# A two-layer decoder trunk on one core: the order of work at the hand-overs between weight strips, and one value strip by the plain product

## The reference, cut to what matters

```python
mem_n = rmsnorm(mem, mem_norm)               # 256 memory tokens
for layer in range(2):
    h = rmsnorm(x, g[0])
    # layer 0: proj = h @ w_in -> q, k, v, u; stick-breaking attention on q, k, v (4 heads x 256),
    #          pooling mixer on u; both concatenated @ w_out
    # layer 1: proj = h @ w_in -> q, k, v, r, a; g = log_sigmoid(a @ gate_w + gate_b) / 16,
    #          gated linear attention in chunks of 64; its norm, times silu(r), @ w_out
    x = x + rmsnorm(mix, g[1])
    x = x + rmsnorm(cross_attention(rmsnorm(x, g[2]), mem_n, ...), g[3])    # 4 heads x 512
    x = x + rmsnorm((silu(h @ w_gate) * (h @ w_up)) @ w_down, g[5])         # h = rmsnorm(x, g[4])
```

## Time and profile before

| | before |
|---|---|
| median of three runs | 3054.8 us |
| the profiled execution, its own time | 3051.12 us |
| its span, first to last instruction | 3049.4 us |
| mean granted TensorE clock, as a share of 2.4 GHz | 0.978 |
| PE busy | 2901.0 us, 95% of the span |
| DVE busy | 2092.8 us, 69% |
| ACT busy | 1541.1 us, 51% |
| POOL busy | 99.6 us, 3% |
| HBM traffic | 191 GB/s over the span |

### The profile page before, as it was taken

How to read it: one execution, slowest core, us unless ns; L and a number is a source line. 1 busy time by engine, 2 the same in 40 slices (tenths; PEclk the granted TensorE clock), 3 DMA queues, 4 the chain that set the end, 5 groups by cost and what they waited for, 6 DMA issues and landing times. The chain is left out here.

```text
span 3049.4 us, 31694 instructions
## 1 busy us (share of the span) xinstructions
PE 2901.0 (95%) x13070; PEld 2398.4 (79%) x13070; DVE 2092.8 (69%) x1376; ACT 1541.1 (51%) x1361; POOL 99.6 (3%) x112
## 2 busy tenths in 40 slices
PE   6999999998899999999998969998999999999998
PEld 5888787787787888887887858777777888887887
DVE  6888776547447888885445858646645988886544
ACT  4666555445335566664444545444434655665443
POOL 0000000001001000000002000001001000000000
PEclk9999999999999999999999969999999999999999
DMA  7665744654454566556554424754535455665552
GB/s 262 221 255 183 279 155 149 235 172 140 184 166 168 205 221 221 192 183 260 193 193 155 166 82 156 262 207 150 195 138 193 178 184 205 221 221 203 211 193 97
DMA packets 237984, 583.44 MB, mean 191 GB/s; under 512 B 8720, under 2 KB 8736, under 8 KB 222096
## 3 DMA queue, kind: packets, MB, share of 16 engines
q1 hardware_dynamic: 232608, 530.61, 49.0%
q0 software_dynamic: 4064, 38.21, 3.2%
q10 hardware_dynamic: 1168, 12.59, 1.0%
HBM read 564.60 MB, written 16.78 MB: 191 GB/s over the span
## 5 line engine op out<-in xcount | busy, mean ns | idle before, releaser
L999 DVE TENSOR_TENSOR w_lo<-wide,w_hi 128x2048 fp32r<-128x2048 f32 x552 | 1255.9, 2289 | 529.7 <-ACT w_hi L542 527.9
L542 ACT ACTIVATE w_hi<-wide 128x2048 fp32r<-128x2048 f32 x552 | 1053.2, 1914 | 559.8 <-PE ps L1547 456.4
L1547 PE MATMUL ps<-w_hi,act_hi 128*128 128x512 f32 x3312 | 1215.4, 393 | 39.0 <-DVE act_lo L1141 22.5
L1547 PE MATMUL ps<-w_lo,act_hi 128*128 128x512 f32 x3312 | 1209.2, 391 | 0.0
L1547 PE MATMUL ps<-w_hi,act_lo 128*128 128x512 f32 x3312 | 1208.7, 391 | 0.0
L1547 PEld LDWEIGHTS ps<-w_hi,act_hi 128*128 128x128 f32 x3312 | 626.3, 189 | 175.5 <-issue 27.8
L1547 PEld LDWEIGHTS ps<-w_hi,act_lo 128*128 128x128 f32 x3312 | 625.4, 189 | 131.4
L1547 PEld LDWEIGHTS ps<-w_lo,act_hi 128*128 128x128 f32 x3312 | 626.3, 189 | 129.1 <-issue 0.2
L1003 DVE TENSOR_TENSOR wide<-wide,wide 128x2048 f32<-128x2048 f32 x108 | 247.2, 2289 | 5.5 <-DVE w_sum L1003 0.5
L1547 PE MATMUL ps<-w_hi,s_hi_x 128*128 128x512 f32 x544 | 217.5, 400 | 23.8 <-ACT ps L592 18.3
L1547 PE MATMUL ps<-w_hi,s_lo_x 128*128 128x512 f32 x544 | 214.4, 394 | 0.0
(11 more groups left out here) (211 smaller groups left out, 1424.6 us busy)
## 6 DMA issues: line engine op xcount, KB each, us to landing
wide<-in_ffn_w_gate SPq DMA_DIRECT2D x88, 1024.0 KB, 7.5
wide<-in_ffn_w_up SPq DMA_DIRECT2D x88, 1024.0 KB, 7.2
wide<-in_ffn_w_down SPq DMA_DIRECT2D x88, 1024.0 KB, 4.8
wide<-in_odd_w_in SPq DMA_DIRECT2D x48, 1024.0 KB, 5.2
wide<-in_xattn_wk SPq DMA_DIRECT2D x32, 1024.0 KB, 8.0
wide<-in_xattn_wv SPq DMA_DIRECT2D x32, 1024.0 KB, 7.0
wide<-in_even_w_in SPq DMA_DIRECT2D x32, 1024.0 KB, 7.1
wide<-in_xattn_wq SPq DMA_DIRECT2D x32, 1024.0 KB, 5.1
```

Source lines behind the costliest of these rows:

```text
L542: nc.scalar.activation(w_hi[:, c % W_SLOTS, :], src, ACT.Copy).then_inc(hi_done, 2)
L999: nc.vector.tensor_tensor(w_lo[:, c % W_SLOTS, :], src, w_hi[:, c % W_SLOTS, :].bitcast(F32), ALU.subtract).then_inc(lo_done, 2)
L1547: return nc.tensor.matmul(dst, lhs, rhs, start=start, stop=stop, skip_group_check=loose)
```

## The change

It does six things:

- The turn of the scale vectors becomes the first work of PE, and its copy the first of DVE.
- In the five stages that go through `transposed`, ACT takes both token halves of a plain strip (`take_both`). In all seven stages the token additions move behind the low part of chunk 7, and `token_hi` and `token_lo` behind chunk 0 of the next strip.
- The scores of the first mixer move inside `sb_vu`'s first strip, behind its chunk c+3. ACT's copies of them come ahead of c+9, Abs to Ln behind c+10, and DVE's join behind chunk 0 of the next strip. The last turn of `sb_qk` moves behind that strip's chunk c.
- `gla_v`'s first strip becomes plain. `state_gates` comes behind chunk 0 of the second strip and `chunk_forms` behind its chunk 3.
- The last `take_t` of `xq` moves ahead of chunk 3 of the next strip (`closes`).
- `band` less one moves ahead of c+7 of `sb_vu`'s first strip on DVE.

```diff
@@ the plan
+    stage("vec", rounds=1)
     stage("mem_norm", rounds=2)
...
-    stage("vec", rounds=1)
...
-            stage("gla_v", (True, True))
+            stage("gla_v", (False, True))
@@ ACT
+            def take_both(st, q, reuse=()):
+                def run():
+                    for m in range(MT):
+                        if m == 0:
+                            act.wait_ge(m0_done, st.a + q + 1)
...
+                        else:
+                            act.wait_ge(w_used, st.c + 4 * q + 4 + W_SLOTS)
+                        nc.scalar.activation(nat[:, q, m, :], ps[:, 2 * q + m, :], ACT.Copy)\
+                            .then_inc(bank_free[2 * q + m], 1)
+                return run
...
-                        rest8(st, before_5, take_m0(st, 0, nat[:, 0, 0, :], reuse=reuse(0)))
-                        if i == 0 and name in SUM_STAGES:
-                            token_hi(name)
-                        lead(nx, take_t(0), take_m0(st, 1, nat[:, 1, 0, :], reuse=reuse(1)))
+                        rest8(st, before_5, take_both(st, 0, reuse(0)))
+                        lead(nx, lambda: (token_hi(name), take_t(0)()), take_both(st, 1, reuse(1)))
...
-                             take_t(0))
+                             (lambda: (take_t(0)(), take_t(1)())) if closes and i == 1 else take_t(0))
...
+                    natural(vu_strips[0], vu, 0, vu_strips[1], take_k, before_9=scores, at_end=soft_plus)
...
-                    natural(v_strips[0], gv, 0, v_strips[1], exp_state)
+                    natural(v_strips[0], gv, 0, v_strips[1], before_1=exp_state)
...
-                token_hi(f"gu{l}")
-                lead(gu[1])
+                lead(gu[1], lambda: token_hi(f"gu{l}"))
@@ DVE
-                            rest8(st, before_5, lambda: (token_adds(name, token_free(name)), own()))
-                            token_lo(name)
...
-                        lead(nx, take_t(0), take_m1(st, 1, nat[:, 1, 1, :], reuse(1)))
+                        rest8(st, before_5)
+                        token_adds(name, token_free(name))
+                        lead(nx, lambda: (token_lo(name), take_t(0)()))
...
+                if st.g is None:
+                    rest8(st, before_5, take_m1(st, 0, dst[:, 1, col:col + NB]))
+                    lead(nxt, before_1, take_m1(st, 1, dst[:, 1, right]))
+                    at_end()
+                    return
...
             first = strip_of("mk0")
+            dve.wait_ge(work_full[4], plan["vec"]["rf"] + 1)
+            nc.vector.tensor_copy(vec[:], ps[:, 4, 0:16]).then_inc(vec_done, 1)
...
-                    transposed("sb_qk", qk, vu_strips[0])()
-                    dve.wait_ge(l_done, 1)
...
+                    take_k = transposed("sb_qk", qk, vu_strips[0])
...
+                    natural(vu_strips[0], vu, 0, vu_strips[1], take_k, band_less_one, soft_plus)
...
-                    natural(v_strips[0], gv, 0, v_strips[1], state_gates, chunk_forms)
+                    natural(v_strips[0], gv, 0, v_strips[1], before_1=state_gates, at_end=chunk_forms)
...
-                rest8(gu[0], before_7=lambda: token_adds(f"gu{l}", token_free(f"gu{l}")))
-                token_lo(f"gu{l}")
-                lead(gu[1], before_3=times_up)
+                rest8(gu[0])
+                token_adds(f"gu{l}", token_free(f"gu{l}"))
+                lead(gu[1], lambda: token_lo(f"gu{l}"), times_up)
@@ PE
             pe.wait_ge(consts_done, 4)
+            pe.wait_ge(small_in, 32)
+            emptied(4, plan["vec"])
+            mm(ps[:, 4, 0:16], vec_rows[0:16, :], ident[0:16, 0:16]).then_inc(work_full[4], 1)
...
-                    transposed("sb_qk", "pre_mix0", "sb_qk")()
...
+                    rest = transposed("sb_qk", "pre_mix0", "sb_qk")
...
-                    strip11(vu_strips[0], "sb_qk")
+                    strip11(vu_strips[0], "sb_qk", after_0=rest, after_3=scores)
...
-                    for st in plan["gla_v"]["strips"]:
-                        strip11(st, "gla_qk")
+                    v0, v1 = plan["gla_v"]["strips"]
+                    quad(v0, 0)
+                    quad(v0, 1)
+                    strip11(v1, "gla_qk")
```

More of the change, by code:

```diff
@@ L657, in take_m0, with transposed @@
                 return run
[L659 removed]
+            def take_both(st, q, reuse=()):
[3 more added lines that the diff above has]
+                            act.wait_ge(m0_done, st.a + q + 1)
+                            for free in reuse:
+                                act.wait_ge(*free)
+                        else:
[3 more added lines that the diff above has]
+                return run
+            def transposed(name, dst, nxt, before_5=nothing, closes=False):
                 pl = plan[name]
@@ L791, in _, with scores, soft_plus @@
                     vu_strips = plan["sb_vu"]["strips"]
-                    transposed("sb_qk", qk, vu_strips[0])()
-                    pl = plan["sb_z"]
+                    take_k = transposed("sb_qk", qk, vu_strips[0])
                     for s_kv in kv_out:
                         act.wait_ge(s_kv, 16)
[L797 to L808, removed]
+                    def scores():
+                        for h in range(SBH):
+                            act.wait_ge(work_full[WORK + h], plan["sb_z"]["rf"] + 1)
+                            nc.scalar.activation(zs[:, h, :], ps[:, WORK + h, 0:384], ACT.Copy, scale=SBD ** -0.5)\
+                                .then_inc(z_done, 1)
+                            act.wait_ge(z_done, h + 1)
+                            act.sem_inc(bank_free[WORK + h], 1)
+                    def soft_plus():
+                        act.wait_ge(z_masked, 2)
+                        then(nc.scalar.activation(sp_t[:], zs[:], ACT.Abs))
+                        then(nc.scalar.activation(sp_t[:], sp_t[:], ACT.Exp, scale=-1.0))
+                        nc.scalar.activation(sp_t[:], sp_t[:], ACT.Ln, bias=1.0).then_inc(l_done, 1)
+                    natural(vu_strips[0], vu, 0, vu_strips[1], take_k, before_9=scores, at_end=soft_plus)
                     act.wait_ge(w_log, SBH)
@@ L1151, in take_m1, with transposed @@
                 return run
-            def transposed(name, dst, nxt, before_5=nothing, before_last=nothing):
+            def transposed(name, dst, nxt, before_5=nothing, closes=False):
                 pl = plan[name]
@@ L1318, in _, with band_less_one, soft_plus @@
                     vu_strips = plan["sb_vu"]["strips"]
-                    transposed("sb_qk", qk, vu_strips[0])()
-                    dve.wait_ge(l_done, 1)
[L1322 to L1327, removed]
-                                                ident[:].unsqueeze(1).broadcast_to([P, 4, P]), ALU.subtract)\
-                            .then_inc(band_done, 1)
-                    natural(vu_strips[0], vu, 0, vu_strips[1])
+                    take_k = transposed("sb_qk", qk, vu_strips[0])
+                    def band_less_one():
+                        dve.wait_ge(consts_done, 8)
+                        for k in range(MT):
+                            part = band[:, :, k, k * P:(k + 1) * P]
+                            nc.vector.tensor_tensor(part, part, ident[:].unsqueeze(1).broadcast_to([P, 4, P]),
+                                                    ALU.subtract).then_inc(band_done, 1)
+                    def soft_plus():
+                        dve.wait_ge(l_done, 1)
+                        nc.vector.scalar_tensor_tensor(out=sp_t[:], in0=zs[:], scalar=0.0, in1=sp_t[:],
+                                                       op0=ALU.max, op1=ALU.add).then_inc(sp_done, 1)
+                    natural(vu_strips[0], vu, 0, vu_strips[1], take_k, band_less_one, soft_plus)
                     pl = plan["sb_sum"]
```

59 lines of the change are left out of this document (27 added, 32 removed).

## The result

The changed kernel takes 3001.7 us, median of four runs (2999.51 to 3005.6), against 3053.2 us before in the same session: a ratio of **0.9835 [0.9817, 0.9852]**, estimated from all the runs (the two medians alone give 0.9831). The forecast was 3005 in 2986 to 3027, so it held. The profiled execution took 2999.51 us with a span of 2997.8, where that of before had 3049.4: 51.6 us less. The sum of the prediction was 49.5.

What follows compares the result with a forecast made beforehand. PE's matmuls bound the kernel (busy 2901.0 of 3049.4 us), leaving its idle time and lower-clock stretches to win. Terms sum to 49.5: 3051.12 profiled becomes 3001.6, median 3.7 above, so 3005 us; range 2986 to 3027.

Steps and rivals of the forecast that it cites:

- Part 1: Scale vectors first: layer 0's products start at about 374.0, second transposes at 382.2 instead of 386.36; gain 4.2 us.
- the other case: Where layer 0 begins, the clock still falls in the 2.9 us that PE idles: gain only 1 us.
- Part 2: Token sums behind the low part: five `transposed` stages gain 15.9 us; two `gu` stages lose 4.0.
- the bound of 7.4: Upper bound of the loss at the two `gu` stages, with one more fall of the clock each.
- Part 3: First mixer's scores inside `sb_vu`'s first strip: stretch 104.9 to 97.0 us, new 3.7 us wait for `snap` 1; gain 8.
- Part 4: `gla_v`'s first strip plain: 112.7 to 98.7 us despite waits of 2.6 and 7.4 and 2.7 for clock; gain 14.
- Part 5: Cross-attention queries closed early, both layers: each 2.3 us of wait and 3.4 of clock; gain 11.4 us.
- The moved arithmetic waits as long as before: Chains of parts 3 and 4 some links longer, both gains at their lower bounds: 3022 us; chance 0.18.
- No new waits: No new waits and a clock that stays up: parts 3 and 4 give 5 and 10 us more, 2990; chance 0.12.
- The change doesn't do what it says at the sums: ACT, in order, copies the second token half late and PE waits on: 3021 us; chance 0.02.
- The feed-forward inherits the 2 us: DVE never regains the `gu` lateness; 20 summed strips each wait 2.0 us at c+1: 3075 us; chance 0.02.

Runs made afterwards that it cites:

- the changed kernel's second run: The changed kernel run again with no edit: 3002.6 us, 0.9832 of the kernel before, span 3000.5 us.
- the run with the loads behind `x`: Changed kernel with the two scale-vector loads issued behind the 2 MB load of `x`: 3009.6 us, 0.9854 of the kernel before.
- later Exp: Changed kernel with ACT's Exp of the first mixer's weights moved to ahead of chunk c+9 of `sb_vu`'s second strip: 2999.8 us, 0.9822 of before.
- forms behind the strip: Changed kernel with `chunk_forms`, `state_queries`, `decayed_queries` and ACT's query exponent moved behind layer 1's second value strip: 3001.9 us, 0.9828 of before.
- value strip summed: Changed kernel with `gla_v`'s first strip summed again, state gates and chunk forms in their old places: 3022.9 us, 0.9897 of before.
- the last run: Changed kernel with three edits together: mixer weights' Exp later, gated-attention forms behind their strip, `gu` sums back: 2987.5 us, 0.978 of before.

## Why the prediction was right

Each term is measured as the shift of the same operation between the two profiled executions, ahead of and behind the part. It is one execution of each kernel, so a fall of the clock that comes in one and not in the other stands in the term.

| part | forecast | measured | by its own reversal (median, span) |
|---|---|---|---|
| 1 vectors | 4.2 | 4.0 | 2.2, 3.4 |
| 2 five token sums | 15.9 | 18.0 (3.0, 4.3, 4.0, 4.1, 2.6) | 20.8, 20.4 |
| 2 `gu` | -4.0 | -2.4 (-0.4, -2.0) | -5.7, -5.7 |
| 3 scores | 8 | 8.4 | 8.6, 8.6 |
| 4 plain value strip | 14 | 14.3 | 20.3, 21.6 |
| 5 closings | 11.4 | 9.4 (4.6, 4.8) | 12.3, 10.8 |
| sum | 49.5 | 51.7 | |

The mechanisms were right; that the sum came within 2.1 us is in part luck. The terms missed by +2.1, +1.6, +0.4, +0.3, -0.2 and -2.0, and offset each other. And outside the parts the changed kernel's execution has a fall of the clock (0.76 over 578.5 to 585.5) where that of before has none, which costs 1.7, and none at the cross-attention of layer 1, where that of before has one (0.68 over 2216 to 2221), which gives 1.7 back.

**Part 1, right in this execution, by luck with the clock.** The start moved by 0.03 us (first product at 24.26, before at 24.29). PE took up its products at 371.06, behind 3.43 us in which it waited for ACT and DVE: the forecast said 2.9. The wait became only 1.0 shorter; the other 3.0 of the 4.0 are clock, which in the kernel before had fallen (0.72 over 371 to 383) and in this execution stays up. The forecast counted on that and put the other case at its lower bound. The other case is the usual one. The wait of 3.4 us is the same in all eleven kernels with the vectors first, and over the seven microseconds from PE's restart the clock is 1.00 in three of them and 0.55 to 0.79 in eight, the changed kernel's second run (0.76) among them. Where it falls 1.7 us or more of the 4.0 are lost again. On the loads row and rule part: the vectors were usable at 14.7 to 15.5 us in these runs and at 22.0 behind 2 MB more, so the "about 2.0 us" of the Trainium skill (DMA: Bandwidth & Descriptors, Anatomy of one DMA — SWDGE (gpsimd) path) does not tell when a small load behind large ones arrives. The page gives that figure for loads issued by GpSimd, and ACT issues these. The prediction's rows decided rightly, but they count packets by size and name no queue; that the order of issue decides is shown by the run with the loads behind `x`.

**Part 2, right.** The idle part was exact, 12.5 us, and so were the two falls of the clock, at `sb_qk` and the first `xq`. What makes 18.0 of 15.9 is for the most part a third fall, at 1662 to 1667 (a clock of 0.66 before), and that one is not the sums' work: it lies 24 us ahead of that stage's wait for `nat` (1687.46), and it is there again in three kernels that have the sums in their new place (later Exp, forms behind the strip, value strip summed), with 0.72 over six microseconds:

```profile
1636.00:1642.00 6.00, 6.00 (x28) 5.23 (x28) 2.58 (x4) 2.28 (x4) 0.00 (x0) 0.72 1.06 358
```

(later Exp). Without it the part gave 16.3. The reversal gave more, because in its execution the clock fell behind four of the five waits and at further places. At `gu` the wait was forecast exactly, 1.1 + 2.0 = 3.1, but in layer 0 the kernel before had a fall of the clock earlier in that stretch (0.66 from 938 to 943), and the changed one's profiled execution had none, which hid 1.7 of the 2.0. The reversal shows the price with its clock, 5.7: beyond the 4.0 and inside the bound of 7.4.

**Part 3, right.** A wait of 3.3 us for 3.7, in the forecast place, and 96.6 us for the stretch against 97.0. ACT's Exp ahead of the `snap`s makes it: moved, the wait is 0.56.

**Part 4, right in the sum, its last two waits wrong.** The wait ahead of the second quad is 2.75 (forecast 2.6), that at c+4 4.93 (5.1). The waits of 1.2 and 1.1 behind `state_queries` and `decayed_queries` did not come. The step that failed is the one that had PE at full speed behind c+4: it made 19 matmuls, 4.3 us at full speed, in 7.04 busy us, and DVE was done in time. That is the 2.7 counted for the clock; the 2.3 counted for waits did not come on top. (That the slower PE is what let DVE be in time follows from the order of the two, and was not tried.) What filled their place is a fall behind the first wait, 0.94 over 29.5 us or 1.8, for which the sum had nothing.

```profile
1771.50:1801.00 29.50, 29.38 (x123) 24.16 (x124) 26.98 (x14) 16.09 (x12) 0.00 (x0) 0.94 0.41 143
...
1809.90:1818.10 8.20, 7.04 (x19) 5.59 (x20) 8.07 (x6) 6.73 (x7) 0.00 (x0) 0.59 0.88 302
```

**Part 5, right, its clock over-counted.** 2.4 us of wait for each closing (3.28 to 0.88) against 2.3, and the clock did stay up, 1.00 for 0.54. But it gave 4.6 - 2.4 = 2.2 and 4.8 - 2.4 = 2.4, not 3.4 each. The step that failed is (1 - 0.54) x 7.5: PE was busy for only 4.85 of those 7.5 us, and a low clock costs nothing while PE idles anyway. Half of 4.85 is 2.4.

**The rivals.** *The moved arithmetic waits as long as before* fell: 3.3 and 4.9 us are in place of 3.3 and 15. *No new waits* fell too, but it is what the last run comes to: with the two chains taken out, 2987.5, where that rival had 2990; but that run has `gu` undone too, for which the rival still paid 4.0. *The change doesn't do what it says at the sums* fell with the wait for `nat`. *The feed-forward inherits the 2 us* fell: no wait at c+1 stands in any later strip, and DVE regained its lateness within one, as the earlier trace rows allowed.

The median came 3.3 us under the forecast: 2.1 from the sum, and the rest because I had put the median 3.7 us above the profiled execution and it was 2.2.

## What to carry to other kernels

Where the engines' orders are written by hand, ask of each transfer of work not how long it is, but which copy stands behind it in its queue and who waits for that copy: at five hand-overs the additions went behind the last thing that the bound engine needs, and the copy that it waits for went to the less busy engine; that took 12.5 us of waits without removing one of the additions. Where the additions alone were moved, in the feed-forward, the kernel lost 5.7 us. Price the granted clock with each wait: a closing that waited 2.4 us less was worth 4.6 to 4.8, and the clock is to be charged on PE's busy time alone. Do not count on a clock that stays up behind a wait of 3 us that remains. And judge a small edit first by the length of its own stage, where 7.8 and 4.7 us could be read that the total time did not show, then put the edits together before dropping one.

## What the runs showed of the hardware

That an idle gap lowers the clock was expected. Not expected was that **the same gap lowers it or not**. PE's wait at `times_up` in layer 0 is 3.14 us in the changed kernel's first run, in its second run, with the later Exp and with the later forms. These are the windows of seven microseconds from PE's restart in each of the four, in this order:

```profile
955.00:962.00 7.00, 7.00 (x31) 5.80 (x32) 7.00 (x4) 4.68 (x6) 0.00 (x0) 1.00 0.11 26
```

```profile
956.40:963.40 7.00, 7.00 (x25) 5.71 (x26) 7.00 (x4) 3.44 (x3) 0.00 (x0) 0.80 0.14 19
```

```profile
951.60:958.60 7.00, 7.00 (x18) 5.54 (x19) 7.00 (x4) 2.52 (x3) 0.00 (x0) 0.56 0.13 17
```

```profile
956.10:963.10 7.00, 7.00 (x19) 5.53 (x20) 7.00 (x4) 2.52 (x3) 0.00 (x0) 0.57 0.14 21
```

PE made 31 matmuls in the first, 25 in the second, 18 and 19 in the others: the same code and the same wait cost nothing, (1 - 0.80) x 7 = 1.4 us or (1 - 0.56) x 7 = 3.1 us of clock. The first two are the same kernel. The wait of 3.43 us where layer 0 begins is a second case, with clocks from 0.55 to 1.00 behind it in eleven kernels (part 1 above). There are about thirty gaps of 1 to 4 us in an execution, so edits that are right in their stage differ at the end by several us. Of the 2.7 us between the two executions of the changed kernel 1.4 are here and 1.7 where layer 0 begins; the falls at other places nearly cancel. The Trainium skill (TensorE: Matmul & The Clock Gate, Part 1: The HAM clock gate) says that the chip's count of activity runs on freely and does not restart with a kernel. By that, what a gap does would depend on when it comes. The windows agree with it; that it is the cause was not tried by itself, and a run that shifts one gap by a known pause would show it.
